# Expert weights in 2 MB transfers of four neighbouring rows, ring slots taken and released in pairs

## The chip, the cores and the metric

One core of a Trainium2 chip runs the whole program. The core has TensorE (PE, matrix multiply, with its weight load shown apart as PEld), VectorE (DVE), ScalarE (ACT), GpSimd (POOL) and SyncE (SP, which here does nothing but issue transfers), and 16 DMA engines that bring data from HBM into the on-chip memory of 128 partitions. The metric is the device time of one execution in microseconds; lower is better.

## The reference

A two-layer encoder trunk on 256 tokens of width 1024, all in float32. Layer 0 mixes tokens with an mLSTM, layer 1 with sliding-window attention; after each mixer comes a mixture of 16 experts, of which every token uses two:

```
for layer in range(2):
    mix = mlstm(h) if layer == 0 else attention(h, shared k and v)
    h = layer_norm(ALPHA * h + mix)
    gate = top-2 weights of softmax(h @ w_router)       # 256 x 16, 14 of 16 zero
    for e in range(16):
        g, u = split(h @ w_gu[layer, e])                # 1024 x 1024
        out += gate[:, e] * ((silu(g) * u) @ w_down[layer, e])   # 512 x 1024
    h = layer_norm(ALPHA * h + out)
```

The weights of one expert are 4 MB (w_gu) and 2 MB (w_down); with 32 experts and the mixers' matrices the program reads some 230 MB.

## The kernel before

Five engines run hand-written instruction streams that meet at semaphores. Every large weight goes through `ring`, 22 slots of 1 MB (8 KB on each partition: two rows of 1024 numbers). Slots are used in one fixed order. The numbers are given by constants: 0 to 3 hold the q and k weights, 4 to 7 V, 8 to 11 O, 12 to 15 w_out_a, 16 to 111 layer 0's experts, 112 and 113 the shared K/V weights, 114 to 121 w_q_b and w_out_b, and 122 to 217 layer 1's experts. Slot number i lies in ring place i % 22. An expert has four slots of w_gu (`u_gu(l, u)`) and two of w_down (`u_dn(l, u)`). Expert 14 of layer 0 has its w_down in slots 108 and 109, expert 15 its w_gu in 104 to 107 and its w_down in 110 and 111.

SP walks through the slots in that order. Before it issues slot i it waits in `free_slot` until PE has counted the semaphore `freed` up to i - 21, that is until the slot 22 places earlier has been used up. PE waits in `need(i)` for the semaphore of that ring place. It adds one to `freed` after the last matmul that reads a slot. So SP can run ahead of PE by the 22 slots, and at the start of each MoE stage the ring is full.

A MoE stage of PE goes: router (L535), building of token lists, four `gather` groups of eight matmuls (L571) that bring the tokens of the first four experts together, and then for each expert `gate_up(u)` (32 matmuls at L587, eight to a slot) and `down(u)` (16 matmuls at L613, eight to a slot). In between stand further gathers for the next four experts (L569, written as transposes against the selection table), `turn_table` (L601) and `scatter` (L625). `down(u)` comes one expert behind: gate_up(15), down(14), then down(15). `turn` (L381) transposes a token tile of h, or of the mixer's val, in 128-column blocks into hT.

The contraction over 1024 inputs is cut into eight k of 128. Any assignment of rows to (k, partition) does if the weights and the activations use the same one. The weights use neighbouring rows on one partition, for long runs in HBM; the activations follow with a stepped read, `rows_of`, which L381, L569 and L571 use for the operand that LDWEIGHTS loads (a `pb<-ident,h` row names first the streamed operand, then the loaded one):

```
def rows_of(src, t, k):
    return src[:, t, k // 2 * 256:(k // 2 + 1) * 256].rearrange("p (n j) -> p j n", j=2)[:, k % 2]
```

Of the kernel before, what the change touches and what calls it, by code (L numbers as in the profile page):

```python
# [11 lines left out]
SEQ, D = 256, 1024  # L12
# [39 lines left out]
def build(nc, x, w_in_a, b_gates_a, mh_norm_a, w_out_a, w_kv_shared, w_q_b, sinks_b, w_out_b,  # L52
          w_router, b_router, w_gu, w_down, ln_g, ln_b, rope, out):
    ctx = ExitStack()
    with ctx:
# [7 lines left out]
        ring = [sb(f"ring{n}", [P, 2, D]) for n in range(RING)]  # L63
# [38 lines left out]
        q_rot = [bufA[:, 0:1024], ring[U_KV % RING][:, 0, :]]  # L102
# [48 lines left out]
        ring_in = [sem(f"ring_in{n}") for n in range(RING)]  # L151
# [50 lines left out]
        def slot(i):  # L202
            return ring[i % RING], ring_in[i % RING]
# [9 lines left out]
        def _(sp):  # L213
            def free_slot(i):

                if i >= RING:
                    sp.wait_ge(freed, i - RING + 1)
                if i == U_KV + RING:
                    sp.wait_ge(qT_done, 4)

            def load(i0, src):

                v = src.rearrange("(q p j) n -> p q j n", p=P, j=2)
                for q in range(src.shape[0] // 256):
                    buf, got = slot(i0 + q)
                    free_slot(i0 + q)
                    sp.dma_start(buf[:, :, :], v[:, q]).then_inc(got, 16)

            def load_down(i0, src):

                v = src.rearrange("(p q j) n -> p q j n", q=2, j=2)
                for q in range(2):
                    buf, got = slot(i0 + q)
                    free_slot(i0 + q)
                    sp.dma_start(buf[:, :, :], v[:, q]).then_inc(got, 16)

            def load_by_head(i0, src):

                v = src.rearrange("(k p) n -> p k n", p=P)
                for q in range(4):  # L240
                    buf, got = slot(i0 + q)
                    free_slot(i0 + q)
                    sp.dma_start(buf[:, :, :], v[:, 2 * q:2 * q + 2, :]).then_inc(got, 16)

            def spill(l):
# [4 lines left out]
                with sp.If(rounds > 0):  # L250
                    sp.wait_ge(s["dve"], 1)
                    with sp.Fori(0, rounds) as j:
                        with sp.Fori(0, EXPERTS) as e:
                            n0 = (j * EXPERTS + e) * (KC + FC)
                            for k in range(KC + FC):
# [3 lines left out]
                                if k < KC:  # L259
                                    src = w_gu[l, bass.ds(e, 1), kk // 2 * 256:(kk // 2 + 1) * 256, :].rearrange(  # L260
                                        "a (p j) n -> j (a p) n", j=2)[kk % 2]
# [8 lines left out]
            for q in range(4):  # L270
                buf, got = slot(U_QK + q)
                for j in range(2):
                    sp.dma_start(buf[:, :, :].rearrange("p k (b n) -> p (k b) n", n=256).rearrange("p (a j) n -> p a j n", j=2)[:, :, j],
                                 w_in[:, q * 256:(q + 1) * 256].rearrange("(a p j) n -> p a j n", p=P, j=2)[:, :, j]
# [9 lines left out]
            for q in range(2):  # L284
                buf, got = slot(U_KV + q)
                free_slot(U_KV + q)
                sp.dma_start(buf[:, :, :].rearrange("p a (b n) -> p (a b) n", b=2).rearrange("p (a j) n -> p a j n", j=2),
                             w_kv_shared.rearrange("(a p j) n -> p a j n", p=P, j=2)[:, 2 * q:2 * q + 2]).then_inc(got, 16)
# [77 lines left out]
        def _(pe):  # L366
            mm = nc.tensor.matmul

            def need(i):

                pe.wait_ge(ring_in[i % RING], landed(i))

            def rows_of(src, t, k):

                return src[:, t, k // 2 * 256:(k // 2 + 1) * 256].rearrange("p (n j) -> p j n", j=2)[:, k % 2]
# [26 lines left out]
            def project(i0, t, c, bank, done, between={}, frees=False):  # L402


                for k in range(KC):
                    if k in between:
                        between[k]()
                    if t == 0 and c == 0 and k % 2 == 0:
                        need(i0 + k // 2)
                    last = mm(pb[bank][:, :], hT[:, k, t * P:(t + 1) * P],  # L410
                              slot(i0 + k // 2)[0][:, k % 2, c * HALF:(c + 1) * HALF], start=k == 0, stop=k == KC - 1)
# [29 lines left out]
            for g in range(8):  # L441

                if g % 2 == 0:
                    need(U_QK + g // 2)
                wqk = slot(U_QK + g // 2)[0][:, :, :].rearrange("p k (b n) -> p (k b) n", n=256)
# [1075 lines left out]
```

## Time and profile before

| | |
|---|---|
| three runs | 697.72 us median (695.93 to 699.08) |
| the profiled execution | 698.31 us, its span from first to last instruction 696.6 us |
| PE, DVE, ACT busy | 656.5, 277.3 and 139.8 us |
| HBM read | 229.85 MB |
| mean granted TensorE clock | 0.990 of full speed |

The profile gives for each engine its busy time, the waits and what ended them, and for each transfer its issue by SP and its landing. "GB/s" is what the 16 DMA engines moved in a stretch. The chain of waits follows the program back from its last instruction, at each step to what released it.

### The profile page before, as it was taken

How to read it: one execution, taken by the hardware profiler on the slowest of the kernel's cores; microseconds unless marked ns; L12 is line 12 of the kernel's file. 1: busy time of each engine (PE TensorE's matmuls, PEld its weight loads, DVE VectorE, ACT ScalarE, POOL GpSimd, SP SyncE). 2: the span in 40 equal slices, each digit the busy share in tenths (PEclk: the TensorE clock that was granted, in tenths of full speed). 3: DMA queues.
4: the chain of work that ended last, by engine and by line, in shares of the span. 5: the costliest groups of instructions: out<-in, count | busy, mean ns of one | idle time of the engine just before them, and what ended most of it. 6: DMA issues, size and time to landing. Idle time of an engine off the chain costs nothing.

```text
span 696.6 us, 7050 instructions
## 1 busy us (share of the span) xinstructions
PE 656.5 (94%) x2750; PEld 291.5 (42%) x2750; DVE 277.3 (40%) x708; ACT 139.8 (20%) x320; POOL 23.0 (3%) x44
## 2 busy tenths in 40 slices
PE   5999999999999999999979998999999999999973
PEld 4864564455333333333224454555333333333321
DVE  0010203345435345353545345456253535335356
ACT  1021334112121121111123041402121121121113
POOL 2300100000000000000000011200000000000000
PEclk9999999999999999999999999999999999999997
DMA  9999903261999999999999970832899999999981
GB/s 281 380 420 421 380 1 147 95 241 34 421 419 422 422 422 422 420 422 421 419 418 412 422 297 22 342 135 108 320 422 420 422 421 421 422 421 422 420 352 62
DMA packets 42166, 231.40 MB, mean 332 GB/s; under 512 B 8073, under 2 KB 12169, under 8 KB 16530
## 3 DMA queue, kind: packets, MB, share of 16 engines
q1 hardware_dynamic: 37696, 230.70, 80.9%
q10 hardware_dynamic: 4434, 0.21, 0.5%
q8 instruction: 23, 0.38, 0.2%
q14 instruction: 13, 0.11, 0.0%
HBM read 229.85 MB, written 1.05 MB: 331 GB/s over the span
## 4 chain that ended last, share of the span: by engine, by line
PE 81%; DMA 8%; DVE 5%; ACT 2%; POOL 1%; ACTq 1%; issue 1%; SPq 0%; POOLq 0%; DVEq 0%
PE pb L587 28%; PE pb L410 17%; PE pb L613 14%; DMA ring<-in_w_down 8%; PE pb L447 4%; PE pb L625 4%; PE pb L732 2%; PE pb L569 2%; PE pb L571 1%; PE pb L381 1%; PE pb L535 1%; PE pb L388 1%; PE pb L498 1%; DVE bufA L1307 1%; POOL bufA L362 1%
## 5 line engine op out<-in xcount | busy, mean ns | idle before, releaser
L410 PE MATMUL pb<-ring,hT 128*128 128x512 f32 x320 | 141.3, 595 | 0.8 <-DVE hT L1470 0.8
L613 PE MATMUL pb<-ring,bufC 128*64 128x512 f32 x512 | 117.1, 597 | 4.3 <-DMA ring<-in_w_down 2.4
L587 PE MATMUL pb<-ring,hT 128*64 128x512 f32 x512 | 114.8, 594 | 3.7 <-DMA ring<-in_w_gu 3.7
L587 PE MATMUL pb<-ring,bufB 128*64 128x512 f32 x512 | 113.2, 593 | 1.9 <-DVE bufC L1290 1.9
L1281 DVE STREAM_TRANSPOSE bufC<-bufC 32x128 f32<-32x128 f32 x256 | 102.9, 402 | 3.8
L1307 DVE COPY bufA<-pb 32x512 f32<-32x512 f32 x64 | 43.7, 683 | 120.2 <-PE pb L613 119.8
L410 PEld LDWEIGHTS pb<-ring,hT 128*128 128x128 f32 x320 | 59.5, 190 | 70.7 <-issue 68.7
L587 PEld LDWEIGHTS pb<-ring,hT 128*64 128x64 f32 x512 | 35.9, 137 | 77.2 <-issue 68.9
L587 PEld LDWEIGHTS pb<-ring,bufB 128*64 128x64 f32 x512 | 36.2, 137 | 73.9 <-issue 70.0
L613 PEld LDWEIGHTS pb<-ring,bufC 128*64 128x64 f32 x512 | 35.1, 136 | 73.7 <-issue 67.6
L956 ACT ACTIVATE bufA<-pb 32x512 f32<-32x512 f32 x64 | 37.7, 589 | 125.3 <-PE pb L613 124.9
L1290 DVE TENSOR_TENSOR bufC<-bufC,pb 128x256 f32<-128x256 f32 x32 | 13.5, 421 | 96.8 <-ACT bufC L962 96.8
L962 ACT ACTIVATE bufC<-pb 128x256 f32<-128x256 f32 x32 | 12.3, 383 | 192.8 <-PE pb L587 192.8
L447 PE MATMUL pb<-hT,ring 128*128 128x256 f32 x128 | 30.7, 406 | 3.2 <-ACT hT L858 3.2
L625 PE MATMUL pb<-bufA,v_shift 128*128 128x512 f32 x64 | 29.6, 605 | 1.9 <-DVE bufA L1307 1.9
L447 PEld LDWEIGHTS pb<-hT,ring 128*128 128x128 f32 x128 | 26.2, 206 | 7.7 <-ACT hT L858 3.6
L362 POOL TENSOR_TENSOR bufA<-bufA,st 128x512 f32<-128x512 f32 x8 | 8.1, 1039 | 359.4 <-DVE st L1459 359.4
L625 PEld LDWEIGHTS pb<-bufA,v_shift 128*128 128x128 f32 x64 | 11.5, 189 | 19.2 <-issue 16.4
L569 PEld LDWEIGHTS pb<-bufC,h 128*128 128x128 f32 x96 | 12.4, 208 | 9.7 <-issue 9.7
L381 PE MATMUL pb<-ident,h 128*128 128x128 f32 x64 | 11.2, 326 | 5.2 <-DMA h<-in_x 4.4
L732 PE MATMUL pb<-ring,hT 128*128 128x512 f32 x32 | 14.2, 595 | 0.8 <-ACT hT L858 0.8
L858 ACT ACTIVATE hT<-pb 128x512 f32<-128x512 f32 x15 | 8.3, 594 | 32.0 <-PE pb L381 31.9
(210 smaller groups left out, 415.8 us busy)
## 6 DMA issues: line engine op xcount, KB each, us to landing
ring<-in_w_gu SPq DMA_DIRECT2D x128, 1024.0 KB, 24.4
ring<-in_w_down SPq DMA_DIRECT2D x64, 1024.0 KB, 26.1
ring<-in_w_in_a SPq DMA_DIRECT2D x8, 1024.0 KB, 18.3
ring<-in_w_in_a SPq DMA_DIRECT2D x8, 512.0 KB, 10.2
ring<-in_w_out_a SPq DMA_DIRECT2D x4, 1024.0 KB, 18.9
ring<-in_w_q_b SPq DMA_DIRECT2D x4, 1024.0 KB, 23.9
ring<-in_w_out_b SPq DMA_DIRECT2D x4, 1024.0 KB, 23.3
ring<-in_w_kv_shared SPq DMA_DIRECT2D x2, 1024.0 KB, 27.6
```

The source lines that it names most:

```text
L362: nc.gpsimd.tensor_tensor(p3, p3, st[:, o + 16:o + 20].rearrange("p (s o) -> p s o", o=1).to_broadcast([P, 4, P]), ALU.mult).then_inc(pn_r ...
L381: last = nc.tensor.transpose(pb[bank0 + 2 * t + j][:, kk * P:(kk + 1) * P], rows_of(src, t, k), ident[:, :])
L410: last = mm(pb[bank][:, :], hT[:, k, t * P:(t + 1) * P], slot(i0 + k // 2)[0][:, k % 2, c * HALF:(c + 1) * HALF], start=k == 0, stop=k == ...
L447: last = mm(pb[g // 2][:, (g % 2) * SEQ:(g % 2 + 1) * SEQ], wqk[:, k, (g % 2) * P:(g % 2 + 1) * P], hT[:, k, :], start=k == 0, stop=k == K ...
L569: last = nc.tensor.transpose(to, rows_of(h, t, k), table)
L587: last = mm(pb[0][c * 64:(c + 1) * 64, :].rearrange("p (a n) -> p a n", a=2), xe[m % 2][:, k, g * SLOTS:(g + 1) * SLOTS], slot(u_gu(l, u) ...
L613: last = mm(pb[2][c * 64:(c + 1) * 64, :], heT[u == EXPERTS - 1][:, (2 * hf + j) * 64:(2 * hf + j + 1) * 64], w[:, j, c * HALF:(c + 1) * H ...
L625: ins = mm(pb[4 + 2 * t + c][:, :], back[:, t * P:(t + 1) * P], ye[t][:, c * HALF:(c + 1) * HALF], start=False, stop=m == QUADS - 1, skip_ ...
L732: last = mm(pb[4 + t][:, :], hT[:, k, t * P:(t + 1) * P], kvw[:, k % 4, :], start=k == 0, stop=k == KC - 1)
L956: last = A(ye[t][g * BLOCK:(g + 1) * BLOCK, HALF:2 * HALF], pb[2][64 + t * BLOCK:64 + (t + 1) * BLOCK, :], ACT.Copy)
L1281: last = V.transpose(heT[to][q_out:q_out + 32, :].rearrange("p (k s) -> p k s", k=FC)[:, :, t * BLOCK:(t + 1) * BLOCK], act_g[n][q_in:q_in ...
L1307: last = V.tensor_copy(ye[t][g * BLOCK:(g + 1) * BLOCK, 0:HALF], pb[2][t * BLOCK:(t + 1) * BLOCK, :])
```

## The change

The ring becomes one tensor, and its places are loaded, waited for and released in pairs. A transfer of a pair brings 2 MB, with four neighbouring rows of the matrix on each partition (16 KB in one run where the matrix is 1024 wide; V and O are column ranges of a wider matrix and keep runs of 4 KB; w_out_b keeps its assignment by heads and 4 KB runs). The q and k weights come in transfers of 1 MB with runs of 2 KB where it was 512 KB with 1 KB. SP waits for both slots of the pair 22 earlier. PE waits once per pair. PE still counts `freed` up once per slot. Since four neighbouring rows now lie on a partition, rows_of reads every fourth element. The small router and gate weights follow in the same assignment.

```
-        ring = [sb(f"ring{n}", [P, 2, D]) for n in range(RING)]
+        ring = sb("ring", [P, RING, 2, D])
...
-        ring_in = [sem(f"ring_in{n}") for n in range(RING)]
+        ring_in = [sem(f"ring_in{n}") for n in range(RING // 2)]
...
+        def pair(i):
+            return ring[:, i % RING:i % RING + 2], ring_in[i % RING // 2]
...
-            def free_slot(i):
+            def free_pair(i):
                 if i >= RING:
-                    sp.wait_ge(freed, i - RING + 1)
+                    sp.wait_ge(freed, i - RING + 2)
...
-                v = src.rearrange("(q p j) n -> p q j n", p=P, j=2)
-                for q in range(src.shape[0] // 256):
-                    buf, got = slot(i0 + q)
-                    free_slot(i0 + q)
-                    sp.dma_start(buf[:, :, :], v[:, q]).then_inc(got, 16)
+                v = src.rearrange("(q p j) n -> p q j n", p=P, j=4)
+                for q in range(2):
+                    buf, got = pair(i0 + 2 * q)
+                    free_pair(i0 + 2 * q)
+                    sp.dma_start(buf[:, :, :, :].rearrange("p u j n -> p (u j) n"), v[:, q]).then_inc(got, 16)
...
             def need(i):
-                pe.wait_ge(ring_in[i % RING], landed(i))
+                pe.wait_ge(ring_in[i % RING // 2], landed(i))
             def rows_of(src, t, k):
-                return src[:, t, k // 2 * 256:(k // 2 + 1) * 256].rearrange("p (n j) -> p j n", j=2)[:, k % 2]
+                return src[:, t, k // 4 * 512:(k // 4 + 1) * 512].rearrange("p (n j) -> p j n", j=4)[:, k % 4]
...
-                        if k % 2 == 0:
+                        if k % 4 == 0:
                             need(u_gu(l, u) + k // 2)
...
                     for hf in range(2):
-                        w = slot(u_dn(l, u) + hf)[0]
-                        need(u_dn(l, u) + hf)
+                        w = slot(u_dn(l, u) + hf)
+                        if hf == 0:
+                            need(u_dn(l, u))
```

On PE, at the start of layer 0's experts, each semaphore `ring_in` stands ahead of four matmuls in gate_up and in down. Before:

```order
L571 MATMUL pb<-bufC,h 128x128 [waits x_sb]
L571 MATMUL pb<-bufC,h 128x128 x3
L587 MATMUL pb<-ring,bufB 64x512 [waits x_sb,ring_in16,he_ready]
L587 MATMUL pb<-ring,bufB 64x512 x3
L587 MATMUL pb<-ring,bufB 64x512 [waits ring_in17]
L587 MATMUL pb<-ring,bufB 64x512 x3
L587 MATMUL pb<-ring,bufB 64x512 [waits x_sb,ring_in18]
L587 MATMUL pb<-ring,bufB 64x512 x3
L587 MATMUL pb<-ring,bufB 64x512 [waits ring_in19]
L587 MATMUL pb<-ring,bufB 64x512 x3
```

And of the changed kernel, at the same place, through gate_up(0) and the first wait of gate_up(1):

```order
L572 MATMUL pb<-bufC,h 128x128 [waits x_sb]
L572 MATMUL pb<-bufC,h 128x128 x3
L588 MATMUL pb<-ring,bufB 64x512 [waits x_sb,ring_in8,he_ready]
L588 MATMUL pb<-ring,bufB 64x512 x7
L588 MATMUL pb<-ring,bufB 64x512 [waits x_sb,ring_in9]
L588 MATMUL pb<-ring,bufB 64x512 x7
L588 MATMUL pb<-ring,bufB 64x512 [waits ring_in10,he_ready]
L588 MATMUL pb<-ring,bufB 64x512 x7
```

No matmul has moved; a wait stands ahead of eight instructions of the listing where it stood ahead of four. The listing has a float32 matmul once that the trace shows as two instructions (L571, L587, L613, L410), so x8 here is 16 there; transposes (L381, L569) count once in both.

On SP, from the first transfers to layer 0's second expert. Before:

```order
L273 DMA ring<-in_w_in_a 128x4x256 x8
L227 DMA ring<-in_w_in_a 128x2x1024 x8
L227 DMA ring<-in_w_out_a 128x2048 x4
L227 DMA ring<-in_w_gu 128x2048 x6
L227 DMA ring<-in_w_gu 128x2048 [waits freed] x2
L235 DMA ring<-in_w_down 128x2048 [waits freed] x2
```

And of the changed kernel:

```order
L275 DMA ring<-in_w_in_a 128x4x512 x4
L231 DMA ring<-in_w_in_a 128x4x1024 x4
L231 DMA ring<-in_w_out_a 128x4096 x2
L231 DMA ring<-in_w_gu 128x4096 x3
L231 DMA ring<-in_w_gu 128x4096 [waits freed]
L237 DMA ring<-in_w_down 128x4096 [waits freed]
```

The order of the matrices is the same; two transfers have become one of twice the size, and two waits for `freed` one.

## Rows read from the trace of the kernel before

**Rows 1.** The page: busy time, and GB/s in 40 slices of the span.

```profile
PE 656.5 (94%) x2750; PEld 291.5 (42%) x2750; DVE 277.3 (40%) x708; ACT 139.8 (20%) x320; POOL 23.0 (3%) x44
...
GB/s 281 380 420 421 380 1 147 95 241 34 421 419 422 422 422 422 420 422 421 419 418 412 422 297 22 342 135 108 320 422 420 422 421 421 422 421 422 420 352 62
```

**Rows 2.** Chain of waits, end of layer 0's experts: start us, us, what.

```profile
327.94 26.41 DMA ring<-in_w_down
```

**Rows 3.** PE's timeline there: start us, us, operation [idle before <-releaser].

```profile
342.20 1.89 PE L587 MATMUL pb<-ring,hT 128*64 128x512 f32 x8
344.45 1.94 PE L587 MATMUL pb<-ring,hT 128*64 128x512 f32 x8 [0.37 <-DMA ring<-in_w_gu]
...
349.43 1.94 PE L587 MATMUL pb<-ring,hT 128*64 128x512 f32 x8 [0.55 <-DMA ring<-in_w_gu]
352.01 1.94 PE L613 MATMUL pb<-ring,bufC 128*64 128x512 f32 x8 [0.64 <-DMA ring<-in_w_down]
354.40 1.94 PE L613 MATMUL pb<-ring,bufC 128*64 128x512 f32 x8 [0.46 <-DMA ring<-in_w_down]
...
357.87 3.65 PE L613 MATMUL pb<-ring,bufC 128*64 128x512 f32 x16 [0.94 <-DVE bufA L1307]
```

**Rows 4.** PE's waits, 165 to 375 us: us in total, times, longest.

```profile
PE pb L587 <- DMA ring<-in_w_gu: 1.5, 3, 0.6
PE pb L613 <- DMA ring<-in_w_down: 1.1, 2, 0.6
```

**Rows 5.** PE's waits, 480 to 697 us.

```profile
PE pb L587 <- DMA ring<-in_w_gu: 2.2, 4, 0.7
PE pb L613 <- DMA ring<-in_w_down: 1.3, 3, 0.6
```

**Rows 6.** Timelines of PE and of SP's issues, start of layer 0's experts.

```profile
169.18 7.09 PE L587 MATMUL pb<-ring,bufB 128*64 128x512 f32 x32
...
171.16 5.48 SPq L227 DMA_DIRECT2D ring<-in_w_gu  x4
```

**Rows 7.** Windows: each engine's busy us (count), PEclk, DMA share, GB/s.

```profile
30.00:39.00 9.00, 9.00 (x43) 7.94 (x42) 0.00 (x0) 0.66 (x2) 0.00 (x0) 1.00 1.03 407
374.00:381.00 7.00, 7.00 (x24) 3.65 (x23) 2.05 (x4) 0.60 (x1) 0.00 (x0) 1.00 1.03 411
190.00:340.00 150.00, 150.00 (x682) 53.29 (x680) 65.76 (x147) 25.63 (x49) 0.00 (x0) 1.00 1.01 421
```

**Rows 8.** SP's issues of q/k weights (first; third and fourth), with landings.

```profile
L273 SPq DMA_DIRECT2D ring<-in_w_in_a x1: 434/434/434, 1.7 to 1.7; - x1
...
DMA to landing us min/median/max: 6.0/6.0/6.0
...
L273 SPq DMA_DIRECT2D ring<-in_w_in_a x2: 571/652/732, 2.7 to 3.4; - x2
...
DMA to landing us min/median/max: 8.5/9.1/9.7
```

**Rows 9.** Timeline of the kernel's start, PE and ACT.

```profile
4.39 3.66 PE L381 MATMUL pb<-ident,h 128*128 128x128 f32 x16 [4.39 <-DMA h<-in_x]
...
8.36 1.28 ACT L858 ACT_TABLE_LOAD   x1 [8.36 <-issue]
...
10.63 0.60 ACT L858 ACTIVATE hT<-pb 128x512 f32<-128x512 f32 x1
...
11.29 30.73 PE L447 MATMUL pb<-hT,ring 128*128 128x256 f32 x128 [3.23 <-ACT hT L858]
```

**Rows 10.** Chain of waits: gathers, step-2 transposes, packed transposes.

```profile
165.22 4.04 PE pb L571 x32
...
377.01 0.95 PE pb L381 x8
...
402.00 0.87 PE pb L742 x8
```

**Rows 11.** Weight loads by form: busy us, mean ns; idle before.

```profile
L569 PEld LDWEIGHTS pb<-bufC,h 128*128 128x128 f32 x96 | 12.4, 208 | 9.7 <-issue 9.7
...
L742 PEld LDWEIGHTS pb<-ident,bufB 128*128 128x128 f32 x8 | 0.9, 140 | 0.5 <-issue 0.5
```

More of the change, by code:

```diff
@@ L100, in build @@
         kdup = bufB[:, 0:1024].rearrange("p (t g d n) -> p t g d n", t=NT, g=A_KV, d=2)
-        q_rot = [bufA[:, 0:1024], ring[U_KV % RING][:, 0, :]]
+        q_rot = [bufA[:, 0:1024], ring[:, U_KV % RING, 0, :]]
         qT = bufB[:, :].rearrange("p (g c r q) -> p g c r q", g=A_KV, c=SEQ // CHUNK, r=2)
@@ L221, in load @@
             def load(i0, src):
[L223 to L235 removed]
+                v = src.rearrange("(q p j) n -> p q j n", p=P, j=4)
[3 more added lines that the diff above has]
+                    sp.dma_start(buf[:, :, :, :].rearrange("p u j n -> p (u j) n"), v[:, q]).then_inc(got, 16)
+            def load_down(i0, src):
+                buf, got = pair(i0)
+                free_pair(i0)
+                sp.dma_start(buf[:, :, :, :].rearrange("p u j n -> p (u j) n"), src.rearrange("(p j) n -> p j n", j=FC)).then_inc(got, 16)
             def load_by_head(i0, src):
                 v = src.rearrange("(k p) n -> p k n", p=P)
[L240 to L243, printed above, removed]
+                for q in range(2):
+                    buf, got = pair(i0 + 2 * q)
+                    free_pair(i0 + 2 * q)
+                    sp.dma_start(buf[:, :, :, :].rearrange("p u j n -> p (u j) n"), v[:, 4 * q:4 * q + 4, :]).then_inc(got, 16)
             def spill(l):
@@ L268, in _ @@
             w_in = w_in_a[0]
[L270 to L274, printed above, removed]
+            for q in range(2):
+                buf, got = pair(U_QK + 2 * q)
+                for a in range(2):
+                    sp.dma_start(buf[:, a].rearrange("p k (b n) -> p (k b) n", b=2),
+                                 w_in[:, q * HALF:(q + 1) * HALF].rearrange("(a p j) n -> p a j n", p=P, j=4)[:, a]
                                  ).then_inc(got, 16)
@@ L283, in _ @@
                 load_down(u_dn(0, u), w_down[0, ORDER[u]])
[L284 to L288, printed above, removed]
+            buf, got = pair(U_KV)
+            free_pair(U_KV)
+            sp.dma_start(buf[:, :, :, :].rearrange("p a k n -> p a (k n)"),
+                         w_kv_shared.rearrange("(a p j) n -> p a (j n)", p=P, j=4)).then_inc(got, 16)
             load(U_Q, w_q_b[0])
@@ L407, in project @@
                         between[k]()
-                    if t == 0 and c == 0 and k % 2 == 0:
+                    if t == 0 and c == 0 and k % 4 == 0:
                         need(i0 + k // 2)
                     last = mm(pb[bank][:, :], hT[:, k, t * P:(t + 1) * P],
-                              slot(i0 + k // 2)[0][:, k % 2, c * HALF:(c + 1) * HALF], start=k == 0, stop=k == KC - 1)
+                              slot(i0 + k // 2)[:, k % 2, c * HALF:(c + 1) * HALF], start=k == 0, stop=k == KC - 1)
                     if frees and k == 0:
@@ L441, in _ @@
             for g in range(8):
-                if g % 2 == 0:
+                if g % 4 == 0:
                     need(U_QK + g // 2)
-                wqk = slot(U_QK + g // 2)[0][:, :, :].rearrange("p k (b n) -> p (k b) n", n=256)
+                wqk = pair(U_QK + g // 4 * 2)[0][:, :, :, :].rearrange("p a k (b n) -> p (a k b) n", n=HALF)
                 for k in range(KC):
-                    last = mm(pb[g // 2][:, (g % 2) * SEQ:(g % 2 + 1) * SEQ], wqk[:, k, (g % 2) * P:(g % 2 + 1) * P],
+                    last = mm(pb[g // 2][:, (g % 2) * SEQ:(g % 2 + 1) * SEQ], wqk[:, k, (g % 4) * P:(g % 4 + 1) * P],
                               hT[:, k, :], start=k == 0, stop=k == KC - 1)
```

26 lines of the change are left out of this document (13 added, 13 removed).

## Prediction

> **What bounds the kernel now.** The page first: TensorE (PE) is busy 94% of the span, the transfers run at about 421 GB/s in both MoE stages and hardly at all just before them [rows 1]. So the share of PE says little about which of the two ends a stage; the chain of waits does. It is PE nearly throughout, but at the end of layer 0's MoE it jumps to a w_down transfer issued at 327.94 us and landed at 354.35 [rows 2]. PE's timeline shows why: the last two experts' rows come 2.4 to 2.5 us apart with 0.4 to 0.6 us of waiting before each, every wait ended by a transfer [rows 3]. PE is fed slot by slot there. All waits on the ring come to 1.5 + 1.1 = 2.6 us in layer 0 [rows 4] and 2.2 + 1.3 = 3.5 us in layer 1 [rows 5]. So both MoE stages are in balance: faster transfers can give back at most 2.6 and 3.5 us, while anything that makes the stream late, or PE slower, shows in the end time. The stream is not free to start early: with the ring full, the first new transfer goes out at 171.16, when the first eight matmuls of the 32 that began at 169.18 are done [rows 6].
>
> **The change, part by part.**
>
> Rate of the transfers. Runs in HBM grow from 8 to 16 KB (MoE, w_out_a, w_q_b); V, O and w_out_b keep 4 KB runs. Stretches with 4 KB runs moved 407 and 411 GB/s, those with 8 KB 421 [rows 7]. Per engine (a sixteenth) a 4 KB run takes 160 ns, an 8 KB run 311, so some 9 ns of each do not grow with size; 16 KB would be 614 ns, 427 GB/s. A slot takes 1.049 MB / 421 = 2.49 us; 72 slots follow the first free one in each layer (number 38 to the second w_down slot of expert 14), 179 us in all; at 427 that is 2.4 us less. Bounds: 0, and what the waits allow.
> The Trainium skill, "DMA: Bandwidth & Descriptors", section Rules for kernel authors, asks for 1 MiB or more per DMA and gives a single 1 MB transfer 78% of the peak; here transfers of that size run at 421 because they are queued behind each other, so the trace does not bear out a gain from size alone. Its Specifications put the ceiling at 435 GB/s, by which a layer's stream would be 5.7 us shorter.
>
> Start of the stream. Two slots must be free, so the first transfer waits for 16 matmuls, not 8: 7.09/4 = 1.77 us later [rows 6]. The next pair is free 3.5 us after it and the transfer lasts 5, so no gap follows. Call it +1.7 us on every landing.
>
> End of the stream. Before, down(14) did its first 8 matmuls at 352.01 while the other slot was in flight, and the second 8 at 354.40 [rows 3]. With one semaphore per pair all 16 start after the second landing: 354.40 + 1.7, and 3.6 us to run, ends at 359.7 against 356.3. So +3.4 us if the rate is unchanged, +1.0 with the 2.4 us of the faster stream. The last pair lands 5 us later, about when the copies to bufA (357.87 before) let down(15) start.
>
> Rows read with a step. rows_of now takes every fourth fp32 of h or val (16 bytes apart) instead of every second as the operand that LDWEIGHTS loads. This the diff hides in two lines, and I take it for the largest item. Eight transposes of a packed operand (L742) take 0.87 us, 109 ns each; eight of a step-2 operand (L381) take 0.95 us, 119 each; 32 gather matmuls at step 2 take 4.04 us [rows 10]. The weight load alone reads 140 ns packed and 208 at step 2 [rows 11]. So at step 2 the load has just become what sets the pace. No row has step 4. Lower bound: nothing more. A middle value: the 10 to 11 ns grow with the step, so 22 more. Upper: at step 2 the load covers 1 KB of the partition in 119 ns; if the distance covered sets the pace, 2 KB take 238, so +119. Step 2 is the nearest row, and that it already sits above the packed pace speaks for a read that is limited by distance; I take +0.12 us each.
> The Trainium skill, "Advanced Engine Details and Errata", section Memory Cachelines, says that SBUF is read in 16-byte lines and that at least two hits on a line are needed to absorb the access latency. By that rule step 2 is nearly free, as the trace agrees, and step 4 is past the edge.
> Where it lands: L381 runs 80 times, L571 64, L569 96. The 16 at the start are hidden: they run at 229 ns each until 8.05 us, and three of the four copies they feed wait for ACT's table load until 9.64 [rows 9]. The other 64 of L381 and the 64 of L571 stand in PE's own line with nothing beside them: 128 x 0.12 = 15.4 us. The 96 of L569 are inside the two streams, 48 each: 5.8 us of PE per layer, of which the 2.6 and 3.5 us of waiting absorb a part, leaving +3.2 and +2.3 [rows 4, 5]. That and the lateness of the stream (+1.0 to +3.4) lie side by side, so the larger counts: 3.2 + 2.3 = 5.5 us with the faster stream, 6.8 without.
>
> Start of the kernel. PE needs 2 MB of q/k weights at 11.29, not 1 [rows 9]. Before, the first half MB landed at 1.71 + 6.0 = 7.7, the fourth at 3.4 + 9.7 = 13.1, 1.8 us apart (290 GB/s with 1 KB runs) [rows 8]. 2 KB runs, by the line through 1 KB (56 ns) and 4 KB (160), take 91 ns: 2.9 us per MB, so 5.9 + 5.8 = 11.7, +0.4 us. Bounds: 0 (at 407 GB/s, 11.1) and 1.8.
>
> SP's and PE's halved number of waits, the allocation of one ring and the reshaped small DMAs on ACT's queue I cost at nothing: SP runs some 26 us ahead of the landings [rows 2], and the router and gate weights are read long after they arrive. If that cover were gone, each such wait would cost a slot, 2.5 us.
>
> Sum: 0.4 + 15.4 + 5.5 = 21.3 us on the profiled execution's 698.3: 719.6. The runs' median is 697.7, half a microsecond lower, well inside their spread.
>
> **Rivals.**
> Step 4 costs little (+22 ns). 128 x 0.022 = 2.8 us; in the streams 1.1 us of PE vanishes in the waits and the stream's lateness decides, +1.0 to +3.4 each. With the start 0.4: +5.2 to +10.0, 703.5 to 708.3. For it: 10 ns is all that the first doubling of the step cost. Against: at step 1 PE, not the load, sets the pace, so 10 ns may hide a larger growth.
> Step 4 is free. +2.4 to +7.2: 700.7 to 705.5.
> The other side: 16 KB runs lift the rate so far that PE never waits, and step 4 is free. The stream's gain must exceed the 3.4 us per layer of lateness, that is 1.9% or 429 GB/s, before anything is won; past 3.3% (435) all 6.1 us of waits go: 698.3 - 6.1 + 0.4 = 692.6. For it: 4 to 8 KB gave 2.5 to 3.4%. Against: a fixed part halves each time, so 1.4% is what follows.
> Step 4 costs far more than the distance, say +0.24 us: 30.7 us in the open, 11.5 per layer less the waits, 17 us: 746.
> That the change does not do what it says (16 KB runs cut back to 8) leaves the lateness and the reads: +3.4 x 2 in place of 5.5, 721.
>
> **How the numbers follow.** Forecast case (715 to 725, the cut-back one in it): 0.53. Small price: 0.22. Free: 0.14, half of it within 0.5% (3.5 us, about what these measurements can tell from no change). Other side: 0.04. Far more: 0.07. Predicted time 719.6. The range takes in the forecast, the small price and the dearer half of the free case: 702.5 to 727. Slower by over 0.5%: 0.53 + 0.22 + 0.07 + 0.07 = 0.89, less 0.02 for causes not seen, 0.87; within: 0.07 + 0.02 = 0.09; faster 0.04.
>
> **What would show it.** L571's 32 gather matmuls at some 7.8 us instead of 4.04, L381's eights at 1.9; weight loads of L569 well above 208 ns. The stream's first issue 3.5 us after gate_up(0) begins, not 1.9. Waits before the last pairs fewer and longer, or gone where PE is late. The rate in mid-stream 421 to 427. The q/k matmuls starting at 11.3 to 12. Wrong would be: step-4 loads near 209 ns (then 701 to 708), or a stream well under 421, which the model has no term for.

## The result, and the profile after

The changed kernel takes 710.45 us (median of 4 runs, 710.08 to 710.77), the kernel before beside it 698.40 (4 runs, 695.93 to 699.36): a ratio of 1.0184 [1.0161, 1.0208]. The profiled execution took 710.08 us, with a span of 708.4 against 696.6, at a mean granted clock of 0.989 against 0.990. So 11.8 us of span have to be found.

The page of the changed kernel, its busy times and its GB/s in 40 slices, answers to [rows 1]:

```profile
PE 664.5 (94%) x2750; PEld 301.3 (43%) x2750; DVE 277.3 (39%) x708; ACT 140.0 (20%) x320; POOL 23.1 (3%) x44
...
GB/s 308 392 424 427 298 1 92 146 216 22 328 428 427 427 428 427 427 428 428 427 427 414 428 249 16 341 105 134 214 432 428 427 425 427 426 428 429 427 325 61
```

The count of instructions on every engine is the same, PE is busy 8.0 us longer and its weight loads 9.8 us longer. The MoE stages' slices read mostly 427 and 428 where they read mostly 419 to 422. The stretch from 190 to 340 us (columns as in [rows 7]):

```profile
190.00:340.00 150.00, 150.00 (x682) 53.41 (x680) 64.46 (x143) 26.72 (x51) 0.00 (x0) 1.00 1.01 428
```

Next the groups of stepped weight loads (busy us, mean ns of one; idle before): two of the changed kernel, the second of which answers to L569 in [rows 11], and then L571 of the kernel before, which the first answers to:

```profile
L572 PEld LDWEIGHTS pb<-bufC,h 128*128 128x128 f32 x64 | 15.1, 329 | 2.3 <-DVE bufC L1269 2.3
L570 PEld LDWEIGHTS pb<-bufC,h 128*128 128x128 f32 x96 | 12.5, 210 | 9.7 <-issue 9.7
```

```profile
L571 PEld LDWEIGHTS pb<-bufC,h 128*128 128x128 f32 x64 | 7.7, 196 | 2.3 <-DVE bufC L1267 2.3
```

And the chain of waits at the gathers and at a tile's turn, as in [rows 10] (start us, us, what):

```profile
168.31 7.73 PE pb L572 x32
...
384.81 0.95 PE pb L382 x8
```

All three groups read h with the same step 4, through the same rows_of. Only L572, the plain float32 matmuls, has become slower: 7.73 us for 32 where it was 4.04, at 329 ns for a load where it was 196. The transposes L382 (before L381) still take 0.95 us for eight, and the loads of the transposes L570 (before L569) 210 ns, against 208.

The start of the changed kernel in ACT's timeline (ACTq is ACT issuing a transfer):

```profile
3.15 1.63 ACTq L852 DMA_DIRECT2D v_shift<-in_w_in_a  x2
4.81 1.81 ACTq L854 DMA_DIRECT2D misc<-in_b_gates_a  x1
6.65 2.34 ACTq L852 DMA_DIRECT2D v_shift<-in_w_in_a  x2
9.02 2.40 ACTq L854 DMA_DIRECT2D misc<-in_b_gates_a  x1
11.46 1.28 ACT L860 ACT_TABLE_LOAD   x1 [11.46 <-issue]
...
13.72 0.60 ACT L860 ACTIVATE hT<-pb 128x512 f32<-128x512 f32 x1
```

and in PE's:

```profile
4.37 3.66 PE L382 MATMUL pb<-ident,h 128*128 128x128 f32 x16 [4.37 <-DMA h<-in_x]
14.38 5.88 PE L448 MATMUL pb<-hT,ring 128*128 128x256 f32 x13 [6.35 <-ACT hT L860]
...
350.70 3.65 PE L588 MATMUL pb<-ring,hT 128*64 128x512 f32 x16 [1.24 <-DMA ring<-in_w_gu]
355.51 3.65 PE L588 MATMUL pb<-ring,hT 128*64 128x512 f32 x16 [1.15 <-DMA ring<-in_w_gu]
360.49 3.65 PE L615 MATMUL pb<-ring,bufC 128*64 128x512 f32 x16 [1.32 <-DMA ring<-in_w_down]
```

Before, the same place in the kernel reads:

```profile
3.14 1.09 ACTq L850 DMA_DIRECT2D v_shift<-in_w_in_a  x2
4.26 0.74 ACTq L852 DMA_DIRECT2D misc<-in_b_gates_a  x1
5.03 1.86 ACTq L850 DMA_DIRECT2D v_shift<-in_w_in_a  x2
6.92 1.42 ACTq L852 DMA_DIRECT2D misc<-in_b_gates_a  x1
```

The q/k matmuls start at 14.38 where they started at 11.29 [rows 9], and what they wait for is ACT's copy of hT, in both kernels. In front of that copy ACT issues six small transfers of the gates (four of weights, two of biases). They took it 5.2 us (3.14 to 8.34) and now 8.3 (3.15 to 11.42), and the table load and the copies stand behind them. At the end of the experts the waits have changed as foreseen: one of 1.2 to 1.3 us before each sixteen matmuls, where it was 0.4 to 0.6 before each eight [rows 3].

Where the span went, from the timelines of PE (a stage is from the start of gate_up(0) to the end of down(14)):

| | before | after | shift |
|---|---|---|---|
| start of the q/k matmuls | 11.29 | 14.38 | +3.1 |
| layer 0: gathers, from the first to gate_up(0) | 3.96 | 7.66 | +3.7 |
| layer 0: stage | 187.1 | 188.1 | +1.0 |
| layer 1: mixer and router | | | +0.8 |
| layer 1: gathers | 3.97 | 7.66 | +3.7 |
| layer 1: stage | 188.45 | 187.95 | -0.5 |
| together | | | +11.8 |

The +0.8 in layer 1's router goes with 3.4 us at a granted clock of half (1.2 GHz), from 484.3 on, that the profiled execution of before doesn't have. Such a stretch comes and goes between the kernels' profiles: of the nine kernels in the experiments below, four have it in layer 1's router too, two have one earlier between the layers (from 379.6 and from 415.3 on), and three have none there. So I ascribe it to no part of the change.

### The profile page after: what moved, and what is told of

Its sections match the earlier page's. It is cut to its first block, busy times and chain, and to the rows that moved or that the text cites. A ratio compares the mean times of both kernels' runs of the same rounds, so it can differ in the third digit from the quotient of the medians.

```text
span 708.4 us, 6938 instructions
## 1 busy us (share of the span) xinstructions
PE 664.5 (94%) x2750; PEld 301.3 (43%) x2750; DVE 277.3 (39%) x708; ACT 140.0 (20%) x320; POOL 23.1 (3%) x44
## 4 chain that ended last, share of the span: by engine, by line
PE 77%; DMA 12%; DVE 5%; ACT 2%; ACTq 1%; POOL 1%; issue 1%; POOLq 0%; DVEq 0%
PE pb L588 24%; PE pb L411 17%; PE pb L615 13%; DMA ring<-in_w_down 12%; PE pb L448 4%; PE pb L627 3%; PE pb L572 2%; PE pb L734 2%; PE pb L570 2%; PE pb L545 1%; PE pb L536 1%; PE pb L382 1%; PE pb L389 1%; PE pb L499 1%; DVE bufA L1309 1%
## 5 line engine op out<-in xcount | busy, mean ns | idle before, releaser
L411 PE MATMUL pb<-ring,hT 128*128 128x512 f32 x320 | 141.3, 595 | 0.8 <-DVE hT L1472 0.8
L570 PEld LDWEIGHTS pb<-bufC,h 128*128 128x128 f32 x96 | 12.5, 210 | 9.7 <-issue 9.7
L572 PE MATMUL pb<-bufC,h 128*128 128x128 f32 x64 | 15.5, 400 | 0.6 <-DVE bufC L1269 0.6
L572 PEld LDWEIGHTS pb<-bufC,h 128*128 128x128 f32 x64 | 15.1, 329 | 2.3 <-DVE bufC L1269 2.3
L382 PE MATMUL pb<-ident,h 128*128 128x128 f32 x64 | 11.2, 327 | 5.1 <-DMA h<-in_x 4.4
## 6 DMA issues: line engine op xcount, KB each, us to landing
ring<-in_w_in_a SPq DMA_DIRECT2D x4, 1024.0 KB, 11.2
```

Source lines behind the costliest of these rows:

```text
L382: last = nc.tensor.transpose(pb[bank0 + 2 * t + j][:, kk * P:(kk + 1) * P], rows_of(src, t, k), ident[:, :])
L411: last = mm(pb[bank][:, :], hT[:, k, t * P:(t + 1) * P], slot(i0 + k // 2)[:, k % 2, c * HALF:(c + 1) * HALF], start=k == 0, stop=k == KC - 1)
L570: last = nc.tensor.transpose(to, rows_of(h, t, k), table)
L572: last = mm(to, rows_of(h, t, k), table, start=True, stop=True)
```

## The experiments

The kernel before was run beside each. Its medians were 698.33 us in the first group (for four kernels: single slots with step 4, pairs with step 2, the gates late, and the steps), 698.54 in the second (for the two-slot release and wait, gates late, and w_down in pairs) and 697.15 in the last.

The main theory after the result was: plain float32 loads with step 4 cost +0.115 us each, 3.7 us a layer, and nothing else in PE's own work changed; ACT's issues cost the start; waiting and releasing by two costs what the prediction said, and the longer runs give most of it back. Rivals: the gathers are slow because of the traffic of the ring and not the step; the size of the transfers and not the length of the runs makes them faster; the start is late because of the 2 MB for which PE waits; distance rather than 16-byte lines sets the price of a step.

**The row assignment alone.** The kernel before, with its single 1 MB slots and 8 KB runs, but rows dealt out in fours. Two slots share one block of 512 rows:

```diff
-                v = src.rearrange("(q p j) n -> p q j n", p=P, j=2)
+                v = src.rearrange("(b p u j) n -> p b u j n", p=P, u=2, j=2)
...
-                    sp.dma_start(buf[:, :, :], v[:, q]).then_inc(got, 16)
+                    sp.dma_start(buf[:, :, :], v[:, q // 2, q % 2]).then_inc(got, 16)
...
-                return src[:, t, k // 2 * 256:(k // 2 + 1) * 256].rearrange("p (n j) -> p j n", j=2)[:, k % 2]
+                return src[:, t, k // 4 * 512:(k // 4 + 1) * 512].rearrange("p (n j) -> p j n", j=4)[:, k % 4]
```

Expected: 

> The kernel before with the changed assignment of rows alone: 1 MB transfers into single slots with single waits and releases as before, runs of 8 KB, but rows_of with a step of four, and the gate weights' small transfers in the changed form. If the step costs the gathers (L571) some 3.7 us a layer and nothing else, as the changed kernel's trace reads: the 64 weight loads of the gathers start 233 ns apart, the transposes (L381, L569) stay at 120, and the time is 698.4 + 7.4 = 705.8 us. If the first q/k matmul's 3.1 us of lateness in the changed kernel come from the form of the small gate transfers, they show here too: start at 14.4 and 708.9 us. If they come from SP's larger transfers ahead of them in the queues, it starts at 11.3. If the gathers' slowdown were not the step but the pairs, the time is 698.4.

Measured: 708.29 us (707.74 to 709.07), 1.0154 [1.0112, 1.0196]. Its chain of waits at layer 0's gathers, and the window from 200 to 320 us:

```profile
165.91 7.73 PE pb L571 x32
```

```profile
200.00:320.00 120.00, 120.00 (x550) 42.75 (x550) 52.76 (x117) 21.84 (x42) 0.00 (x0) 1.00 1.01 421
```

The gathers alone cost what they cost in the changed kernel, to the hundredth, with the ring's transfers as before; transfers and the ring's traffic have no part in it. Two layers make 7.4 us; q/k starts 0.6 us later, at 11.86, and a stretch at half clock from 379.6 on, after layer 0's experts, takes another 1.7. Its stages last 188.7 and 187.7 us. The 705.8 of the expectation counted the gathers alone; the measured time is 2.5 above it.

**Pairs without the row assignment.** The changed kernel, with 2 MB transfers and pairs of slots, but two neighbouring rows on a partition: 8 KB runs in the w_gu transfers, step 2 in rows_of. (w_down, whose assignment already had four neighbours over two slots, comes in 16 KB runs as in the changed kernel. V and O are loaded in 1 MB transfers here.)

```diff
-                v = src.rearrange("(q p j) n -> p q j n", p=P, j=4)
...
-                    sp.dma_start(buf[:, :, :, :].rearrange("p u j n -> p (u j) n"), v[:, q]).then_inc(got, 16)
+                    sp.dma_start(buf[:, :, :, :],
+                                 src[q * 512:(q + 1) * 512].rearrange("(u p j) n -> p u j n", p=P, j=2)).then_inc(got, 16)
...
-                return src[:, t, k // 4 * 512:(k // 4 + 1) * 512].rearrange("p (n j) -> p j n", j=4)[:, k % 4]
+                return src[:, t, k // 2 * 256:(k // 2 + 1) * 256].rearrange("p (n j) -> p j n", j=2)[:, k % 2]
```

Expected: 

> The changed kernel with the old assignment of rows: 2 MB transfers into pairs, pair waits and releases, but step two in rows_of, and w_gu, w_out_a and w_q_b in runs of 8 KB (w_down keeps 16 KB; V and O go in 1 MB transfers). Gathers back at 118 ns apart: 7.4 us less than 710.45. The rate in mid-stream tells run length from number of transfers: 423 GB/s if the run length made the gain (a third of the bytes in 16 KB runs), 427 if the number of transfers did. With the start still 3.1 us late: 703 us at 427, 705 at 423 (0.7 us less gain in each layer). Rival, that the pairs and not the step slow the gathers: 710.

Measured: 705.66 us (704.89 to 706.58), 1.0123 [1.0081, 1.0165]. Chain at the gathers, window, and PE's timeline at the end of layer 0's experts:

```profile
167.24 4.04 PE pb L574 x32
```

```profile
200.00:320.00 120.00, 120.00 (x552) 42.71 (x550) 52.68 (x117) 21.07 (x40) 0.00 (x0) 1.00 1.01 423
```

```profile
352.24 3.65 PE L590 MATMUL pb<-ring,hT 128*64 128x512 f32 x16 [1.22 <-DMA ring<-in_w_gu]
357.23 3.65 PE L617 MATMUL pb<-ring,bufC 128*64 128x512 f32 x16 [1.34 <-DMA ring<-in_w_down]
```

With step 2 the gathers are back at 4.04. The number of transfers in the stages is that of the changed kernel, but the rate is 423 and not 427: two thirds of the bytes still come in 8 KB runs, and the third in 16 KB runs gives some 2 GB/s of the 6. So the length of the run makes the rate, not the size of the transfer. The q/k matmuls start at 13.07. The stages last 189.6 and 189.4 us: handling slots in pairs costs, and the rate pays for some of it.

**ACT's issues behind its copies.** Of the changed kernel, with ACT's gate transfers (the line `act.wait_ge(gate_zero, 2)` and the six issues) moved behind its three copies of hT:

```diff
-            act.wait_ge(gate_zero, 2)
-            for g in range(2):
-                w4 = w_in_a[0, :, 3072 + g * M_HEADS:3072 + (g + 1) * M_HEADS]
...
             def take_hT(n, t, bank0):
...
                 take_hT(0, t, 4)
+            act.wait_ge(gate_zero, 2)
+            for g in range(2):
+                w4 = w_in_a[0, :, 3072 + g * M_HEADS:3072 + (g + 1) * M_HEADS]
```

Expected: 

> The changed kernel, with ACT issuing the six small gate transfers after its three first copies of hT instead of before them. If the 3.1 us at the start are ACT's issues held up (5.2 us of issuing before, 8.3 after), the copies are done by 9.5 us and the first q/k matmul waits for the landing of the first pair at about 12.4 instead: 1.9 us sooner, 708.5 us. If the matmul was bound by the landing of the pair anyway, nothing changes: 710.4. If the gate weights then come late for their own matmuls at 41 us, a wait appears there.

Measured: 707.59 us (704.71 to 708.04), 1.0133 [1.0086, 1.0179], where the changed kernel has 1.0184 [1.0161, 1.0208]; its profiled span is 706.3, against 708.4. PE's timeline:

```profile
12.39 7.89 PE L448 MATMUL pb<-hT,ring 128*128 128x256 f32 x22 [4.46 <-DMA ring<-in_w_in_a]
```

The start comes 2.0 us earlier, and its wait is now for the transfer. So in the changed kernel two things were late at the start: the second transfer of the pair, at 12.4, and ACT's copy, at 14.3, which hid it.

The same move in the kernel before:

Expected: 

> The kernel before with ACT's six gate transfers issued after its three first copies of hT, as in the run on the changed kernel. The first q/k matmul then waits for the first slot's landing at 9.44 us instead of ACT's copies at 11.24: 1.8 us sooner and 696.6 us. If larger transfers of SP, and not the place in ACT's order, were all of the start's delay, nothing is won: 698.4.

Measured: 695.44 us (691.81 to 696.68), 0.9943 [0.9921, 0.9965]. PE's timeline:

```profile
8.75 11.46 PE L447 MATMUL pb<-hT,ring 128*128 128x256 f32 x52 [0.73 <-ACT hT L850]
```

The start moves from 11.29 to 8.75, which is 2.5 of the 3.1 us between the medians. The profiled execution is 3.8 us shorter, because layer 1's stage is 1.8 us shorter in it as well (186.7 against 188.45); stages with an unchanged stream differ by as much from kernel to kernel (table below). It beats both kernels. With the issues moved away in both, the starts are 8.75 and 12.39: 3.6 us, where nothing hides them. Not all of that is waiting for a pair: in this run the second slot had landed at 11.6 (its last transfer was issued at 3.3 and took 8.3), so some 0.8 us go with the changed form of the q/k transfers.

**Steps measured by themselves.** Once, behind layer 0's experts in the kernel before, eight plain float32 matmuls and eight transposes (128 columns each, results unused) for each of six steps s of the loaded operand, as in

```diff
+            for _ in range(8):
+                mm(pb[4][:, 0:P], hTf[:, 0:512].rearrange("p (n s) -> p s n", s=4)[:, 0], ident[:, :], start=True, stop=True)
+            for _ in range(8):
+                nc.tensor.transpose(pb[4][:, 0:P], hTf[:, 0:512].rearrange("p (n s) -> p s n", s=4)[:, 0], ident[:, :])
```

Expected: 

> The kernel before with extra work between the layers: eight plain float32 matmuls and eight transposes at each of the steps 1, 2, 3, 4, 6 and 8 of the loaded operand (hT), the streamed operand being the identity. It measures the disputed cost by itself. If the distance covered sets the pace, as the prediction took it, the plain loads are 118 ns apart at step 2, 177 at 3, 236 at 4, 354 at 6 and 472 at 8, and the transposes the same. If the 16-byte line does, nothing grows beyond step 4: 175 at 3 and 233 at 4, 6 and 8. The changed kernel's trace has transposes at 121 with step 4; if that is a property of the transpose, they stay near 120 at every step from 4 on; if it is one of the operand (h against hT), they do not.

Measured (one execution of 719.04 us, a time that holds some 20 us of added work). The chain of waits through the six steps, at the full granted clock; the first of each two is the plain matmul (16 instructions), the second the transpose (8):

```profile
370.20 1.79 PE pb L725 x16
371.99 0.87 PE pb L727 x8
372.86 1.89 PE pb L729 x16
374.74 0.95 PE pb L731 x8
375.69 2.77 PE pb L733 x16
378.46 0.90 PE pb L735 x8
379.36 3.73 PE pb L737 x16
383.08 0.95 PE pb L739 x8
384.04 3.57 PE pb L741 x16
387.61 1.06 PE pb L743 x8
388.67 3.79 PE pb L745 x16
392.47 0.88 PE pb L747 x8
```

Divided by the counts, in ns per instruction, and the number of 16-byte lines that the 128 values of 4 bytes touch on a partition:

| step | 1 | 2 | 3 | 4 | 6 | 8 |
|---|---|---|---|---|---|---|
| plain matmul | 112 | 118 | 173 | 233 | 223 | 237 |
| 16-byte lines | 32 | 64 | 96 | 128 | 128 | 128 |
| transpose | 109 | 119 | 113 | 119 | 133 | 110 |

The plain matmuls cost 118/64 = 1.84, 173/96 = 1.80 and 233/128 = 1.82 ns for each line, and stop growing once every value has a line of its own (223 and 237 at steps 6 and 8). At step 1 the count of lines asks for 58 ns and the rest of PE's work for 112, so the load is hidden; at step 2 the two are about equal. The distance law of the prediction gives 238 at step 4 as well, but 357 at step 6 and 476 at step 8, and is refuted. The Trainium skill, "Advanced Engine Details and Errata", section Memory Cachelines, says that SBUF, the on-chip memory, is read in lines of 16 bytes; the saturation at step 4 and the even price for a line agree with it.

The transposes follow neither the count of lines nor that section's rule: 109 to 133 ns with no order in it. Their loads by themselves take 141 ns at step 1 and 201 to 243 at the others; those of the plain matmuls take 192 and 196 at steps 1 and 2, 261 at step 3, and 317 to 334 from step 4 on. No run here says why a transpose's load is spared. What the trace shows is a difference in form: the listing's one plain float32 matmul is two instructions in the trace, a transpose one.

**Releasing by two.** The kernel before, with SP waiting for both slots of a pair before it loads either:

```diff
-                    sp.wait_ge(freed, i - RING + 1)
+                    sp.wait_ge(freed, i // 2 * 2 - RING + 2)
```

Expected: 

> The kernel before with one thing of the pairs: SP waits for both slots of a pair before it issues the first of the two 1 MB transfers. The prediction priced it at 1.77 us on every landing of both streams, so the last experts' waits and the end move by as much: 698.4 + 3.5 = 701.9 us, first issue of layer 0's stream at 172.9 instead of 171.16. Rival: the queue is refilled so far ahead that the late start is made good: 698.4.

Measured: 700.91 us (697.24 to 701.49), 1.0030 [1.0014, 1.0046]. SP's timeline:

```profile
173.36 4.24 SPq L227 DMA_DIRECT2D ring<-in_w_gu  x4
```

The first new transfer goes out 3.7 us after gate_up(0) starts, at 169.66, where it was 2.0. That is the 1.7 us of the prediction. PE's waits on the ring from 165 to 375 us:

```profile
PE pb L587 <- DMA ring<-in_w_gu: 2.2, 4, 0.6
PE pb L613 <- DMA ring<-in_w_down: 1.5, 3, 0.6
```

They come to 3.7 us where it was 2.6 [rows 4], and layer 0's stage is 1.5 longer (188.6 against 187.1). In layer 1 the stage is 188.3, against 188.45. The mean of the two is 0.9 above that of the kernels whose stream is unchanged. The stages alone don't prove it: the kernel with step 4 alone, whose stream is unchanged, waited the same 3.7 us in layer 0, and its stage there lasted 188.7. What is clear of noise is the time, 2.4 us or 0.3% longer. Of the 2.6 us between the two profiled executions, 1.4 stand in the stages. The other 1.2 stand ahead of the two layers' gathers, where this execution has stretches at half clock (from 11.2, 76.1 and 478.9 on) that the one of before doesn't have.

**Waiting by two.** The kernel before, with PE waiting for both slots of a pair:

```diff
-                pe.wait_ge(ring_in[i % RING], landed(i))
+                if i % 2 == 0:
+                    pe.wait_ge(ring_in[i % RING], landed(i))
+                    pe.wait_ge(ring_in[(i + 1) % RING], landed(i + 1))
```

Expected: 

> The kernel before with the other half of the pairs: PE waits once for both slots of a pair (1 MB transfers, single releases). down(14) then does its 16 matmuls after the second landing instead of 8 of them before it: 1.6 us later at the end of each layer, 698.4 + 3.3 = 701.7 us, and the waits of the last two experts are half as many and twice as long. Rival: PE's wait total and not its last wait counts, which does not change: 698.4.

Measured: 704.08 us (700.20 to 705.32), 1.0071 [1.0052, 1.0091]. Timeline at the end of layer 0's experts, with one wait of 1.3 us before sixteen matmuls as in the changed kernel:

```profile
351.74 3.65 PE L589 MATMUL pb<-ring,hT 128*64 128x512 f32 x16 [1.31 <-DMA ring<-in_w_gu]
356.69 3.65 PE L615 MATMUL pb<-ring,bufC 128*64 128x512 f32 x16 [1.31 <-DMA ring<-in_w_down]
```

The stages are 188.9 and 189.3, +1.6 over the unchanged ones. q/k waits until 12.76 for its second slot, +1.5 us, which the expectation did not count. The profiled execution is 5.6 us longer than that of before: 1.5 at the start, 2.6 in the two stages, and 1.5 ahead of the two layers' gathers, where it too has stretches at half clock (from 78.1 and 480.9 on) that the other doesn't have.

How the stages compare (us, layer 0 and layer 1). In one kernel such a stage varies by up to 1.4 us from layer to layer, so single values don't carry a difference of that size; the means of the kernels of one kind do better, though three of them are means of two values:

| stream | kernels | stages | mean |
|---|---|---|---|
| as before | before; step 4 alone; steps; gates late | 186.7 to 188.7 (8) | 187.5 |
| released by two | one | 188.6, 188.3 | 188.4 |
| waited for by two | one | 188.9, 189.3 | 189.1 |
| pairs, 423 GB/s | one | 189.6, 189.4 | 189.5 |
| pairs, 427 GB/s | changed; with gates late | 188.1, 187.95; 188.1, 187.9 | 188.0 |

**w_down alone in pairs.** Since w_down already lay in four neighbouring rows, it can have its 16 KB runs without a step 4 anywhere. The kernel before with the gates late, and w_down of experts 0 to 13 of each layer loaded in one transfer of 2 MB; the last two experts keep single slots for the sake of the end:

```diff
+        paired = {u_dn(l, u) for l in range(2) for u in range(EXPERTS - 2)}
...
+                if i0 in paired:
+                    sp.wait_ge(freed, i0 - RING + 2) if i0 >= RING else None
...
+                    sp.dma_start(ring_all[:, i0 % RING:i0 % RING + 2].rearrange("p u j n -> p (u j) n"),
+                                 src.rearrange("(p j) n -> p j n", j=FC)).then_inc(ring_in[i0 % RING], 16)
+                    return
```

Expected: 

> The same, with the w_down weights alone in 2 MB transfers of 16 KB runs, for all experts but the last two of each layer; w_gu stays in single slots at step two. The gathers stay at 118 ns, the stream starts as early and ends as finely as before, and a third of the bytes go at the longer run: 423 GB/s as in the pairs with 8 KB runs, 0.9 us less stream in each layer. 696.6 - 1.8 = 694.8 us. Rival: the late release of w_down pairs leaves gaps that eat the 0.9 us: 696.6.

Measured: 694.30 us (693.02 to 698.42), 0.9941 [0.9919, 0.9962], not to be told from the 0.9943 without it. The window and the timeline:

```profile
200.00:320.00 120.00, 120.00 (x550) 42.66 (x548) 53.97 (x121) 21.03 (x40) 0.00 (x0) 1.00 1.01 423
```

```profile
339.32 3.65 PE L628 MATMUL pb<-ring,bufC 128*64 128x512 f32 x16 [1.91 <-DMA ring<-in_w_down]
...
346.69 1.94 PE L602 MATMUL pb<-ring,hT 128*64 128x512 f32 x8 [0.28 <-DMA ring<-in_w_gu]
```

The rate rose by 2 GB/s. The pair is waited for whole, 1.91 us here and up to 2.3 in layer 1, before the last experts; the stages are 188.3 and 188.7, where the mean with the stream as before is 187.5. But the profiled execution, 698.42 us, was the slowest of six whose median is 694.30, so these stages may be longer than usual. The medians say only that nothing measurable was won.

**The first gathers as transposes.** The changed kernel with the gates late, with the first gathers written as the later ones are, as transposes against a table (make_perm) that DVE has to build first:

```diff
-                        if m:
-                            last = nc.tensor.transpose(to, rows_of(h, t, k), table)
-                        else:
-                            last = mm(to, rows_of(h, t, k), table, start=True, stop=True)
+                        last = nc.tensor.transpose(to, rows_of(h, t, k), table)
...
-                make_pick(0).then_inc(pick_ready, 1)
                 count_rounds(l)
                 make_dest()
+                make_perm(0).then_inc(pick_ready, 1)
```

Expected: 

> The changed kernel with the late gate transfers, and the first four experts' gathers also written as transposes (16 of them, against a permutation), which VectorE can give out only after its list building, some 3.6 us later in before's trace (pick at 165.2, dest ready at 168.8). Transposes at step four are 121 ns apart, so the gathers take 1.9 us and not 7.7: the way from the first pick to gate_up(0) is some 5.8 us instead of 7.7, and the time is 707.6 - 2 x 1.9 = 703.8 us. If the 16-byte step slowed these loads too, once nothing else stands between them, they would take 3.7 us and the time would be 707.4.

Measured: 709.91 us (707.58 to 712.26), 1.0172 [1.0128, 1.0216]; its profiled span is 708.2, against 706.3 of the kernel it was made from. The expectation, 703.8 us, was missed; the ratio is not clearly above the 1.0133 [1.0086, 1.0179] of that kernel either. PE's timeline, and windows to either side of 175.7 us:

```profile
170.22 3.69 PE L569 MATMUL pb<-bufC,h 128*128 128x128 f32 x16 [4.10 <-DVE bufC L1260]
173.83 4.58 PE L585 MATMUL pb<-ring,bufB 128*64 128x512 f32 x16
```

```profile
169.00:175.70 6.70, 5.48 (x22) 3.92 (x24) 1.03 (x5) 3.53 (x5) 0.00 (x0) 0.50 0.00 0
175.70:180.00 4.30, 4.30 (x24) 1.41 (x22) 0.00 (x0) 0.14 (x1) 0.00 (x0) 1.00 0.25 46
```

The gathers take 3.6 us instead of 7.7, but start 3.8 us later: a chain of some twenty small DVE operations (counting of rounds, then the destinations), which before ran beside the gathers, now stands ahead of them. And while PE idles for 4.1 us its granted clock falls to half, at 168.9, and stays there until 175.7 (in layer 1 from 493.2 to 500.0); the kernel it was made from has no such stretch at either place. So the sixteen transposes run at 226 ns each, not 120, and the first 1.9 us of gate_up(0) at half clock as well. gate_up(0) begins 0.2 us earlier than without the edit, and the stage then lasts 0.8 us longer; in layer 1 the stage is 1.1 longer (187.9 to 189.0). A table built earlier was not tried.

## Why the prediction came out as it did

The direction, the range and the kind of the causes held; the 21.3 us were 11.8. The sum erred both ways: 13.0 us too much for the transposes, the gathers and the streams, 3.5 too little for the start and the clock. The range held because it was wide enough to take in a small price of the step, not because the sum was near. By its own terms:

| term | predicted | measured |
|---|---|---|
| start | +0.4 | +3.1 |
| L381, 64 transposes in the open | +7.7 | 0 |
| L571, 64 gather matmuls in the open | +7.7 | +7.4 |
| the two streams | +5.5 | +0.5 |
| a half-clock stretch in the router | none | +0.8 |
| sum | +21.3 | +11.8 |

**Rows read with a step.** The step that failed is "Step 2 is the nearest row, and that it already sits above the packed pace speaks for a read that is limited by distance; I take +0.12 us each", applied to three lines at once: the term it made was 15.4 us, and 7.4 were measured. For L571 the number was right (7.73 us for 32 against a forecast 7.8) and its reason wrong: a law of 16-byte lines and one of distance give the same at step 4. For L381 and L569 both were wrong, since transposes are not slowed. The two rows that were compared, 109 ns packed and 119 at step 2, were both transposes, so the price was extrapolated from the form of instruction that turned out not to have one. The rule of 16-byte lines in the Trainium skill, "Advanced Engine Details and Errata", section Memory Cachelines, does not tell the two forms apart either. Two of the profile signs that the prediction named were therefore missed: L381's eights stayed at 0.95 us, not 1.9, and the loads of L569 at 210 ns, which the prediction had called the sign that the time would be 701 to 708. That sign was right of two lines of the three.

**The streams.** The term was "the larger counts", PE's 3.2 and 2.3 us for slower transposes. With that gone, the lateness remains, for which the prediction had +1.0 a layer with the faster stream. Measured is +0.5 us a layer against the mean of the unchanged stages, and +1.0 and -0.5 against the two of the kernel before. Its parts, by the table of stages: release +0.9 and wait +1.6, 2.5 together, for the predicted 1.7 + 1.6 (put at 3.4); the wait's size was right. The release makes the first issue 1.7 us later, as forecast (in the changed kernel it goes out at 179.66, 3.7 us after gate_up(0) begins); layer 0's stage then ends 1.5 later than before and layer 1's no later. What absorbs it in layer 1 stays open: the difference is as large as the spread between stages that have the same stream. By the same table, the faster stream gives back 1.5 us a layer from 423 to 427 GB/s, and 2.0 if the release's and the wait's 2.5 are set against the 0.5 that are left; 2.4 was forecast.

**The rate.** "16 KB would be 614 ns, 427 GB/s" was right to the number, 427 to 428. The fixed part of some 9 ns for a run holds through 16 KB, and the two kernels at 423 confirm that the run counts and not the transfer. The 78% for a single 1 MB transfer that the prediction named stand in the Trainium skill, "DMA: Bandwidth & Descriptors", in the section Bandwidth, measured on transfers issued from GpSimd; the ones here are issued by SP. The other side's rival, 435 and more, had no such row.

**The start.** The step "PE needs 2 MB of q/k weights at 11.29 ... 5.9 + 5.8 = 11.7, +0.4 us" was a little low, with the landing at 12.4. What decided was "the reshaped small DMAs on ACT's queue I cost at nothing". I named SP's lead and late readers as the cover, and these cover the data. They do not cover ACT, whose issues stand ahead of the copies that PE waits for. [Rows 9] showed it: the table load at 8.36 with "issue" as what ended the wait, and PE's wait ended by ACT's hT. That the issues grew from 5.2 to 8.3 us is shown; what in the change makes them longer is not. With rows in fours and single slots they took 5.8 us, with pairs and rows in twos 7.0. Two kernels whose transfers are those of before (released by two, waited for by two) show 5.2 and 4.7, so the 5.8 of one profile is hardly outside the spread, while the 7.0 is: the larger transfers have a share, the rows in fours perhaps one beside them.

**The rivals.** "Step 4 costs little" (703.5 to 708.3) had nearly the right sum for the transposes, and the forecast the right one for the gathers. A case with both, a price of nothing for the transposes and 0.12 us for the gathers, would have been 698.3 + 0.4 + 7.7 + 2.0 (the stream's lateness in two layers) = 708.4; the start's further 2.7 and the clock's 0.8 make it 711.9, and the streams' 0.5 in place of 2.0 and the gathers' 7.4 in place of 7.7 the 710.1 of the profiled run. Since I took one price for all three lines, no case stood there.

## What to carry to other kernels

Before a longer run is bought in HBM, count what the reader of the other operand pays: 427 instead of 421 GB/s gave back some 2 us a layer in a stage in balance, and the step of four values that it forced cost 3.7 us a layer in 32 instructions of plain float32 matmuls, while handling the ring in pairs took some 2.5. Price each form of instruction from a row of its own form: going from step 2 to step 4 cost 115 ns in a plain matmul and nothing in a transpose. And where a stage waits for a copy, look at what else that engine issues ahead of it: moving six small transfers behind three copies made the kernel before 0.57% [0.35, 0.79] faster without any other change.

## What the runs showed that I had not expected

- A stepped float32 load costs 1.8 ns for each 16-byte line it touches in a plain matmul (118, 173 and 233 ns at steps 2, 3 and 4, then 223 and 237 at 6 and 8), hidden below 112 ns. A transpose with the same operand stays at 109 to 133 ns.
- The issue of the same number of small transfers by ACT took 4.7 and 5.2 us in kernels with the transfers of before, 5.8 with rows in fours, 7.0 with pairs of slots and 8.3 with both. What holds the issues up is not shown.
- An idle stretch of PE of 4.1 us ahead of the transposes, in both layers, went with 6.8 us at a granted clock of half, begun while PE was still idle, in which a transpose took 226 ns. So the wait in front of a shorter way to the same work can eat what it wins.
